# A gated linear attention's score levels joined in blocks of 1, 4 and 16 tokens, with two pieces of work moved in the queues

## The chip, the cores and the metric

The program runs on one core of one Trainium2 chip. The metric is the device time of one execution in microseconds; the kernel before has a median of 2559.4 us over 3 runs (2558.29 to 2559.68).

## The reference

The whole program is a retention layer, a latent-attention layer, a gated linear attention (GLA) layer with a feed-forward, all in float32. The change touches only the GLA mixer. It has 4 heads, a key width of 128 and a value width of 256 a head, and 1024 tokens:

```python
log_a = jax.nn.log_sigmoid(gk_low @ w_gk_up + b_gk) / 16.0
b = jnp.cumsum(gb, axis=-2)                                  # within a chunk
o_inter = jnp.einsum('bhck,bhkv->bhcv', qb * jnp.exp(b), state)
diff = b[:, :, :, None, :] - b[:, :, None, :, :]
decay = jnp.exp(jnp.where(causal[:, :, None], diff, -jnp.inf))
attn = jnp.einsum('bhik,bhjk,bhijk->bhij', qb, kb, decay)
o_intra = jnp.einsum('bhij,bhjv->bhiv', attn, vb)
k_dec = kb * jnp.exp(b_last - b)
state = state * jnp.exp(b_last) + jnp.einsum('bhck,bhcv->bhkv', k_dec, vb)
```

The kernel takes chunks of 128 tokens. The weight of query i on key j, i > j, is a sum over 128 key channels of q_i k_j exp(b_i - b_j). With a reference token m between them it is a plain product of q_i exp(b_i - b_m) and k_j exp(b_m - b_j), so pairs (i, j) are sorted by the reference token they share, and each sort is a matmul of its own.

## The kernel before

`gla_heads` (line 2074) gives one instruction stream to each of TensorE, VectorE, ScalarE, GpSimd and SyncE, joined by semaphores. `head(h, ...)` is run for the heads h = 0 to 3 (1 and 2 in a loop), and in it the steps t = 0 to 7, one for each chunk of 128 tokens; s = 8h + t. The order within a step is written out by hand.

TensorE (`tensor`, line 2632): in step t it runs `project_vr` of chunk t (24 matmuls of 512 columns, L2600), then `attend` of chunk s-3 (L2611 to L2614), then `scores` of chunk s-2 (L2622 to L2626). In step 4 the gate matmuls of the next head follow (L2580). After step 7 come four groups of 24 matmuls, `project_qk` (L2559), for the next head; the group g >= 2 reuses a bank and waits until ScalarE has copied group g-2 out. `attend(s)` waits for the chunk's weights (`mask_done`), for ScalarE to have copied out the output of chunk s-1 (`o_copied`), and for the state (`R_done`).

`scores` has 7 levels. At level l the 128 tokens of a chunk are cut into pairs of blocks of 2^l tokens, and the last token of the pair's first block is the reference; one 64-column matmul gives all pairs of that level (L2626). The diagonal is the column sum of q times k by a matmul with a matrix of ones (L2622), and the decayed keys are transposed (L2623).

VectorE (`vector`, line 2500): in each step `carry_state`, `gate`, `gather_weights` of chunk s-2, and then at most one or two pieces of the list below. `exponents(h, c)` forms the differences of b for one half c of a head (4 chunks, 512 tokens): 14 TENSOR_TENSOR of 256 elements and one of 512 (L2431 to L2434). ScalarE then runs `exponentials(h, c)` on them (L2260 to L2262), and `products(h, c)` multiplies by q and k (L2446 to L2450, 14 of 256 and 3 of 512). `gather_weights` copies the keys out of PSUM, puts the levels together by predicated copies into two tiles, even and odd, each copy waiting for the last but one, and adds the two tiles (L2475 to L2490).

The order of these pieces in VectorE: steps 0 and 1, `w_lower` (the lower part of a weight split) of pieces 0 and 1 of the next head; step 2, `up_lower`; step 3, `exponents(h, 1)`; step 4, `products(h, 1)`; steps 5 and 6, the gates of the next head; step 7, `exponents(h + 1, 0)`; after step 7, `w_lower` of pieces 2 to 5 and `products(h + 1, 0)`. In the last head steps 0 to 2 and 5 to 7 end instead with a call of `meanwhile`, which does weight splits of the closing stage (L3110 in VectorE, L3048 in ScalarE), one row block in each of the steps 0, 1 and 2.

ScalarE (`scalar`, line 2291): in each step `evacuate` of chunk s (copy of v, SiLU of the gate, L2277 and L2280) and `output` of chunk s-3 (copy of the output out of PSUM, L2287, and its squares, L2289); then `w_upper` in steps 0 and 1, `up_upper` in step 2, `exponentials(h, 1)` in step 3, `log_gates` in step 5, and in the last head `meanwhile` at the very end of a step. After step 7 it runs `w_upper(2)`, `qk_copy(0)`, `exponentials(h + 1, 0)`, `w_upper(3)`, `qk_copy(1)`, `w_upper(4)`, `qk_copy(2)`, `w_upper(5)`, `qk_copy(3)`. SyncE loads the raw weight pieces into two buffers; piece i waits until `w_lower` of piece i-2 is done.

## Time and profile before

| | |
|---|---|
| median of 3 runs | 2559.4 us |
| time of the profiled execution | 2557.12 us |
| span of the profiled execution | 2555.2 us |
| granted TensorE clock, mean | 0.999 |
| TensorE busy | 2523.7 us, 99% of the span |
| VectorE busy | 1220.6 us, 48% |
| ScalarE busy | 921.8 us, 36% |
| GpSimd busy | 466.2 us, 18% |
| mean DMA traffic | 76 GB/s |

The steps of the four GLA heads run from 1407 us to 1762 us of the span. The times of the rows below are microseconds from the start of the span.

### The profile page before, as it was taken

To read this page: it belongs to the slowest core of one execution; us is meant where nothing else is said; L and a number is where in the kernel's file an instruction comes from. 1 tells how busy PE (TensorE), PEld (TensorE's weight loads), DVE (VectorE), ACT (ScalarE), POOL (GpSimd) and SP (SyncE) were. 2 spreads that over 40 slices of the span, in tenths; PEclk is the share of its full clock that TensorE was granted. 3 is DMA by queue.
4 is the path that set the end of the run, shared out by engine and by line. 5 is a ranking of instruction groups with operands and counts; after the bars stand their busy time and mean duration, and the time that the engine had idled before them with its cause. 6 is when DMAs were issued, how large, how long until landed. Compare 5 with 4: busy or idle time off the path is not lost.

```text
span 2555.2 us, 34947 instructions
## 1 busy us (share of the span) xinstructions
PE 2523.7 (99%) x12568; PEld 2129.1 (83%) x12568; DVE 1220.6 (48%) x2485; ACT 921.8 (36%) x1840; POOL 466.2 (18%) x933
## 2 busy tenths in 40 slices
PE   8999999999999999999899999999999999999999
PEld 7888888888888987888788888888888888888887
DVE  4553634536423410577756767765443333333334
ACT  5443433424313422555544535443331122112212
POOL 3453534434000304322010101101000000000001
PEclk9999999999999999999999999999999999999999
DMA  5220211202533221222342111023341111111111
GB/s 212 78 76 21 92 39 58 73 18 93 194 115 106 69 91 52 61 60 60 97 162 99 42 59 45 31 79 110 110 141 40 50 57 41 49 46 61 33 49 75
DMA packets 76232, 194.48 MB, mean 76 GB/s; under 512 B 8528, under 2 KB 29392, under 8 KB 75344
## 3 DMA queue, kind: packets, MB, share of 16 engines
q1 hardware_dynamic: 76112, 192.85, 23.0%
q8 instruction: 79, 1.29, 0.2%
q14 instruction: 41, 0.34, 0.0%
HBM read 152.45 MB, written 36.18 MB: 74 GB/s over the span
## 4 chain that ended last, share of the span: by engine, by line
PE 57%; DVE 2%; ACT 1%; issue 1%; DMA 1%; DVEq 0%; POOL 0%; ACTq 0%; POOLq 0%; SPq 0%
PE wc_g_ps L3461 14%; PE wc_y_ps L3477 14%; PE gl_vr_ps L2600 7%; PE gl_j_ps L2559 3%; PE wb_y_ps L2928 3%; PE wc_y_ps L3210 3%; PE gl_l_ps L2626 2%; PE at_T_ps L1960 1%; PE at_j_ps L1912 1%; PE at_v_ps L1912 1%; PE at_v_ps L1913 1%; PE at_v_ps L1914 1%; PE at_s_ps L1914 1%; PE at_s_ps L1913 1%; PE at_s_ps L1912 1%
## 5 line engine op out<-in xcount | busy, mean ns | idle before, releaser
L3461 PE MATMUL wc_g_ps<-x_upper,ff_w1l 128*128 128x512 f32 x512 | 199.3, 389 | 0.0
L3461 PE MATMUL wc_g_ps<-x_upper,ff_w1h 128*128 128x512 f32 x512 | 199.2, 389 | 0.0
L3477 PE MATMUL wc_y_ps<-ff_w2h,ff_hl 128*128 128x512 f32 x512 | 199.2, 389 | 0.0
L3477 PE MATMUL wc_y_ps<-ff_w2l,ff_hh 128*128 128x512 f32 x512 | 199.2, 389 | 0.0
L3461 PE MATMUL wc_g_ps<-x_lower,ff_w1h 128*128 128x512 f32 x512 | 199.2, 389 | 0.0
L3477 PE MATMUL wc_y_ps<-ff_w2h,ff_hh 128*128 128x512 f32 x512 | 199.2, 389 | 0.0
L3415 DVE TENSOR_TENSOR ff_acc<-wc_y_ps,ff_acc 128x1024 f32<-128x1024 f32 x63 | 77.2, 1225 | 210.8 <-PE wc_y_ps L3477 210.8
L3340 ACT ACTIVATE ff_relu<-wc_g_ps 128x512 f32<-128x512 f32 x64 | 38.3, 598 | 378.8 <-PE wc_g_ps L3461 378.8
L3401 DVE SCALAR_TENSOR_TENSOR wc_g_ps<-wc_g_ps,ff_relu 128x512 f32<-128x512 f32 x64 | 44.8, 700 | 178.6 <-ACT ff_relu L3340 178.6
L3369 POOL TENSOR_SCALAR ff_ms<-ff_ss 128x1 f32<-128x1 f32 x8 | 1.8, 223 | 686.9 <-ACT x_lower L3357 686.0
L3477 PEld LDWEIGHTS wc_y_ps<-ff_w2l,ff_hh 128*128 128x128 f32 x512 | 96.1, 188 | 20.0
L3477 PEld LDWEIGHTS wc_y_ps<-ff_w2h,ff_hl 128*128 128x128 f32 x512 | 96.1, 188 | 20.0
L3461 PEld LDWEIGHTS wc_g_ps<-x_upper,ff_w1h 128*128 128x128 f32 x512 | 96.1, 188 | 20.0
L3461 PEld LDWEIGHTS wc_g_ps<-x_upper,ff_w1l 128*128 128x128 f32 x512 | 96.1, 188 | 19.9
L3461 PEld LDWEIGHTS wc_g_ps<-x_lower,ff_w1h 128*128 128x128 f32 x512 | 96.1, 188 | 19.9
L3477 PEld LDWEIGHTS wc_y_ps<-ff_w2h,ff_hh 128*128 128x128 f32 x512 | 96.1, 188 | 19.9
L1256 PE MATMUL ra_qkv_ps<-ra_wide_h,ra_xl 128*128 128x512 f32 x256 | 104.3, 407 | 8.1 <-DVE ra_wide_l L986 8.1
L1041 DVE TENSOR_TENSOR ra_sT<-ra_s_ps,ra_decay 128x128 f32<-128x128 f32 x64 | 18.6, 291 | 188.0 <-PE ra_s_ps L1295 188.0
L1256 PE MATMUL ra_qkv_ps<-ra_narrow_h,ra_xl 128*128 128x512 f32 x256 | 103.7, 405 | 0.0
L376 PE MATMUL wa_y_ps<-wa_wh,wa_gl 128*128 128x512 f32 x256 | 102.2, 399 | 0.8 <-DVE ra_vl L1061 0.6
L2600 PE MATMUL gl_vr_ps<-gl_vrh,x_lower 128*128 128x512 f32 x256 | 101.7, 397 | 0.0
L1256 PE MATMUL ra_qkv_ps<-ra_wide_h,ra_xh 128*128 128x512 f32 x256 | 101.3, 396 | 0.0
(433 smaller groups left out, 6992.0 us busy)
## 6 DMA issues: line engine op xcount, KB each, us to landing
staging<-in_w_ff SPq DMA_DIRECT2D x64, 512.0 KB, 3.8
...
```

Of the source, the lines that this page charges most:

```text
L376: last = pe.matmul(y_ps[slot][:, c, :], a[:, slot, kt, :], b[kt][:, c * HALF:(c + 1) * HALF], start=(kt == 0 and i == 0), stop=(kt == KW - ...
L1256: last = pe.matmul(out, a[:, kt, t * P:(t + 1) * P], b[:, kt, at:at + HALF], start=(kt == 0 and i == 0), stop=(kt == KT - 1 and i == 2))
L1912: pe.matmul(out, al, bh, start=start, stop=False)
L1913: pe.matmul(out, ah, bl, start=False, stop=False)
L1914: return pe.matmul(out, ah, bh, start=False, stop=stop)
L2559: last = pe.matmul(out, w[:, r, cols], xx[:, r, at], start=(r == 0 and i == 0), stop=(r == KT - 1 and i == 2))
L2600: last = pe.matmul(vr_ps[t % 2][:, :], xx[:, r, t * P:(t + 1) * P], w[:, r, :], start=(r == 0 and i == 0), stop=(r == KT - 1 and i == 2))
L2928: last = pe.matmul(y_ps[t % 2][:, c, :], a[t % 2][:, kt, :], b[kt][:, c * HALF:(c + 1) * HALF], start=(kt == 0 and i == 0), stop=(kt == KW ...
L3210: last = pe.matmul(y_ps[t % 2][:, c, :], a[t % 2][:, kt, :], b[kt][:, c * HALF:(c + 1) * HALF], start=(kt == 0 and i == 0), stop=(kt == KW ...
L3415: dve.tensor_tensor(acc[t][:, :], y_ps[t % 2][:, :, :].rearrange("p a n -> p (a n)"), acc[t][:, :], ALU.add).then_inc(y_added, 1)
L3461: last = pe.matmul(f_ps[j % 2][:, :], a[kt // 2][:, kt % 2, f * P:(f + 1) * P], b[:, kt, half * HALF:(half + 1) * HALF], start=(kt == 0 an ...
L3477: last = pe.matmul(y_ps[t % 2][:, n, :], a[:, f, t * P:(t + 1) * P], b[f][:, n * HALF:(n + 1) * HALF], start=(f == 0 and i == 0), stop=(f ...
```

## The change

Seven levels become three, of block size n = 1, 4 and 16. Each group of 4n tokens has three reference tokens, the last of its first, second and third block. The queries behind reference r are 3-r blocks, so that a level has 96 + 64 + 32 = 192 query columns a chunk, against 128 keys scaled to the end of their own block. At n = 1 the keys need no scale, so that the raw k is used. The last halving, 64 against 64 tokens, stays as it was (`halves`). The diagonal comes from a matmul of raw k and raw q. The chunks 4 to 7 use a copy of q and k (`own_qk`). `gather_weights` has 11 predicated copies in the place of 8. The last-token keys are the tile `gl_lv_rest[1]` and get their exponential in an instruction of their own. `exponents(h, 1)`, `exponentials(h, 1)` and `products(h, 1)` come one step earlier, and after step 7 the weight splits of pieces 2 and 3 stand ahead of `exponents(h + 1, 0)`.

```diff
-    NL = GLA_LEVELS
+    NL = len(GLA_BLOCKS)
+    BY_REF = (0, 96, 160)
+    QUERIES = 192
+    PARTS = 3 * NL + 2
+    LEVEL_AT = (P, P + QUERIES, 0)
+    HALVES_AT, KEYS_AT = QUERIES, QUERIES + GLA_HALF
+    MASK_AT = [3 * sum(P // (4 * m) for m in GLA_BLOCKS[:i]) for i in range(NL + 1)]
...
-    lv_main = [place(f"gl_lv{c}", [P, NL + 1, HALF], F32, at * KB) for c, at in enumerate((148, 112))]
+    EXPONENTS = NL * BT * QUERIES + (NL - 1) * HALF + HALF
+    lv_main = [place(f"gl_lv{c}", [P, EXPONENTS], F32, at * KB) for c, at in enumerate((148, 112))]
+    own_qk = [[place(f"gl_own_{n}{i}", [P, 2, P], F32, at) for i, at in enumerate(ats)]
+              for n, ats in (("q", (194 * KB, 148 * KB + 4 * EXPONENTS)), ("k", (76 * KB + 1568, 112 * KB + 4 * EXPONENTS)))]
     lv_rest = [place(f"gl_lv_rest{c}", [P, 2, HALF], F32, at * KB) for c, at in enumerate((164, 168))]
...
+    def queries(c, level):
+
+        at = level * BT * QUERIES
+        return lv_main[c][:, at:at + BT * QUERIES].rearrange("p (t n) -> p t n", t=BT)
+
+    def keys(c, level):
+
+        at = NL * BT * QUERIES + (level - 1) * HALF
+        return lv_main[c][:, at:at + HALF]
+
+    def halves(c):
+
+        return lv_main[c][:, EXPONENTS - HALF:EXPONENTS]
+    def own_chunk(src, t):
+
+        if t >= NT - 4:
+            return own_qk[src is k][t // 2 - 2][:, t % 2, :]
+        return src[:, t * P:(t + 1) * P]
+
+    def by_reference(c, level, r):
+
+        n = GLA_BLOCKS[level]
+        return queries(c, level)[:, :, BY_REF[r]:BY_REF[r] + 32 * (3 - r)].rearrange("p t (g x) -> p t g x", x=(3 - r) * n)
+
+    def behind_reference(src, level, r):
+
+        n = GLA_BLOCKS[level]
+        return src.rearrange("p (t g x) -> p t g x", t=BT, x=4 * n)[:, :, :, (r + 1) * n:]
...
         def exponentials(h, c):
             act.wait_ge(sub_done, 2 * h + c + 1)
-            act.activation(lv_main[c][:, :, :], lv_main[c][:, :, :], ACT.Exp, scale=INV_NORM)
+            act.activation(lv_main[c][:, :], lv_main[c][:, :], ACT.Exp, scale=INV_NORM)
+            act.activation(lv_rest[c][:, 1, :], lv_rest[c][:, 1, :], ACT.Exp, scale=INV_NORM)
             act.activation(lv_rest[c][:, 0, :], b[:, c * HALF:(c + 1) * HALF], ACT.Exp, scale=INV_NORM)
...
-                if t == 3:
+                if t == 2:
                     exponentials(h, 1)
                 if more and t == 5:
                     log_gates(h + 1)
                 if not more:
                     meanwhile(act, t)
             if more:
-                for g in range(4):
-                    w_upper(h + 1, 2 + g)
-                    qk_copy(h + 1, g)
-                    if g == 0:
-                        exponentials(h + 1, 0)
+                w_upper(h + 1, 2)
+                w_upper(h + 1, 3)
+                qk_copy(h + 1, 0)
+                w_upper(h + 1, 4)
+                exponentials(h + 1, 0)
+                qk_copy(h + 1, 1)
+                w_upper(h + 1, 5)
+                qk_copy(h + 1, 2)
+                qk_copy(h + 1, 3)
...
-                last = dve.tensor_tensor_scan(b[:, at], ones[:, :], mn[:, 0, at], 0.0, ALU.mult, ALU.add)
+                last = dve.tensor_tensor_scan(b[:, at], ones[:, :].broadcast_to([P, P]), mn[:, 0, at], 0.0, ALU.mult, ALU.add)
...
         def exponents(h, c, older):
-            for level in range(NL):
-                n = 1 << level
-                src = b[:, at].rearrange("p (g u n) -> p g u n", u=2, n=n)
-                dst = lv_main[c][:, level, :].rearrange("p (g u n) -> p g u n", u=2, n=n)
-                mid = src[:, :, 0, n - 1:n].broadcast_to([P, HALF // (2 * n), n])
-                dve.tensor_tensor(dst[:, :, 0, :], mid, src[:, :, 0, :], ALU.subtract)
-                dve.tensor_tensor(dst[:, :, 1, :], src[:, :, 1, :], mid, ALU.subtract)
+            for level, n in enumerate(GLA_BLOCKS):
+                if level:
+                    src = b[:, at].rearrange("p (g n) -> p g n", n=n)
+                    dve.tensor_tensor(keys(c, level).rearrange("p (g n) -> p g n", n=n),
+                                      src[:, :, n - 1:n].broadcast_to([P, HALF // n, n]), src, ALU.subtract)
+                for r in range(3):
+                    src = b[:, at].rearrange("p (t g x) -> p t g x", t=BT, x=4 * n)
+                    dve.tensor_tensor(by_reference(c, level, r), behind_reference(b[:, at], level, r),
+                                      src[:, :, :, (r + 1) * n - 1:(r + 1) * n].broadcast_to([P, BT, 32 // n, (3 - r) * n]),
+                                      ALU.subtract)
+            n = GLA_HALF
+            src = b[:, at].rearrange("p (t u n) -> p t u n", u=2, n=n)
+            dst = halves(c).rearrange("p (t u n) -> p t u n", u=2, n=n)
+            mid = src[:, :, 0, n - 1:n].broadcast_to([P, BT, n])
+            dve.tensor_tensor(dst[:, :, 0, :], mid, src[:, :, 0, :], ALU.subtract)
+            dve.tensor_tensor(dst[:, :, 1, :], src[:, :, 1, :], mid, ALU.subtract)
             src = b[:, at].rearrange("p (t n) -> p t n", n=P)
-            dve.tensor_tensor(lv_main[c][:, KD, :].rearrange("p (t n) -> p t n", n=P),
+            dve.tensor_tensor(lv_rest[c][:, 1, :].rearrange("p (t n) -> p t n", n=P),
                               src[:, :, P - 1:P].broadcast_to([P, BT, P]), src, ALU.subtract).then_inc(sub_done, 1)
...
         def products(h, c):
+                if level:
+                    dve.tensor_tensor(keys(c, level), keys(c, level), k[:, at], ALU.mult)
+                for r in range(3):
+                    dst = by_reference(c, level, r)
+                    dve.tensor_tensor(dst, dst, behind_reference(q[:, at], level, r), ALU.mult)
+            dst = halves(c).rearrange("p (t u n) -> p t u n", u=2, n=GLA_HALF)
+            for u, src in enumerate((k, q)):
+                dve.tensor_tensor(dst[:, :, u, :], dst[:, :, u, :],
+                                  src[:, at].rearrange("p (t u n) -> p t u n", u=2, n=GLA_HALF)[:, :, u, :], ALU.mult)
+            if c:
+                for src in (q, k):
+                    for i in range(2):
+                        dve.tensor_copy(own_qk[src is k][i][:, :, :],
+                                        src[:, HALF + 2 * i * P:HALF + 2 * (i + 1) * P].rearrange("p (t n) -> p t n", n=P))
+            dve.tensor_tensor(lv_rest[c][:, 1, :], lv_rest[c][:, 1, :], k[:, at], ALU.mult)
+            dve.tensor_tensor(lv_rest[c][:, 0, :], lv_rest[c][:, 0, :], q[:, at], ALU.mult).then_inc(mul_done, 1)
...
-            dve.tensor_copy(kt_[:, :], T_ps[:, P:2 * P])
-            for i, level in enumerate((0, None, 2, 1, 4, 3, 6, 5)):
-                dst, n = aT_parts[i % 2], 1 << (level or 0)
-                if i >= 2:
-                    dve.wait_ge(part_done, (NL + 1) * s + i - 1)
+            dve.tensor_copy(kt_[:, :], T_ps[:, KEYS_AT:KEYS_AT + P])
+            dve.copy_predicated(aT_parts[0][:, :], ident[:].bitcast(U32), l_ps[:, 0:P]).then_inc(part_done, 1)
+            dve.copy_predicated(aT_parts[1][:, GLA_HALF:], mask[:, MASK_AT[-1]:MASK_AT[-1] + 1].broadcast_to([P, GLA_HALF]),
+                                T_ps[:, HALVES_AT:HALVES_AT + GLA_HALF]).then_inc(part_done, 1)
+            i = 2
+            for level, n in enumerate(GLA_BLOCKS):
+                bank, groups = (l_ps, l_ps, T_ps)[level], P // (4 * n)
+                for r in range(3):
+                    dve.wait_ge(part_done, PARTS * s + i - 1)
                     wait_alone(dve)
-                if level is None:
-                    last = dve.copy_predicated(dst[:, :], ident[:].bitcast(U32), T_ps[:, 0:P])
-                else:
-                    last = dve.copy_predicated(
-                        dst[:, :].rearrange("p (g u n) -> p g u n", u=2, n=n)[:, :, 1, :],
-                        mask[:, level, :].rearrange("p (g n) -> p g n", n=n),
-                        l_ps[:, level * (P // 2):(level + 1) * (P // 2)].rearrange("p (g n) -> p g n", n=n))
-                last.then_inc(part_done, 1)
-            dve.wait_ge(part_done, (NL + 1) * s + NL + 1)
+                    at, x, w = LEVEL_AT[level] + BY_REF[r], (3 - r) * n, MASK_AT[level] + r * groups
+                    dve.copy_predicated(
+                        aT_parts[i % 2][:, :].rearrange("p (g x) -> p g x", x=4 * n)[:, :, (r + 1) * n:],
+                        mask[:, w:w + groups].unsqueeze(2).broadcast_to([P, groups, x]),
+                        bank[:, at:at + groups * x].rearrange("p (g x) -> p g x", x=x)).then_inc(part_done, 1)
+                    i += 1
+            dve.wait_ge(part_done, PARTS * s + PARTS)
             dve.tensor_tensor(aT[:, :], aT_parts[0][:, :], aT_parts[1][:, :], ALU.add).then_inc(mask_done, 1)
...
+                if t == 2:
+                    exponents(h, 1, older)
                 if t == 3:
-                    exponents(h, 1, older)
-                if t == 4:
                     products(h, 1)
                 if more and t == 5:
                     split_gates(h + 1)
                 if more and t == 6:
                     dve.wait_ge(exp_done, 2 * h + 2)
                     sum_gates(h + 1)
-                if more and t == 7:
-                    exponents(h + 1, 0, 1)
                 if not more:
                     meanwhile(dve, t)
             if more:
-                for i in range(2, PIECES):
-                    w_lower(h + 1, i)
+                w_lower(h + 1, 2)
+                w_lower(h + 1, 3)
+                exponents(h + 1, 0, 1)
+                w_lower(h + 1, 4)
+                w_lower(h + 1, 5)
                 products(h + 1, 0)
...
-            pe.matmul(T_ps[:, 0:P], ones[:, :], lv_rest[c][:, 1, at], start=True, stop=True)
-            pe.transpose(T_ps[:, P:2 * P], lv_main[c][:, KD, at], ident[:])
+            qc, kc = own_chunk(q, t), own_chunk(k, t)
+            pe.transpose(T_ps[:, KEYS_AT:KEYS_AT + P], lv_rest[c][:, 1, at], ident[:])
+            pe.matmul(l_ps[:, 0:P], kc, qc, start=True, stop=True)
             for level in range(NL):
-                n = 1 << level
-                last = pe.matmul(l_ps[:, level * (P // 2):(level + 1) * (P // 2)].rearrange("p (g n) -> p g n", n=n),
-                                 lv_main[c][:, level, at],
-                                 lv_main[c][:, level, at].rearrange("p (g u n) -> p g u n", u=2, n=n)[:, :, 1, :],
-                                 start=True, stop=True)
+                pe.matmul((l_ps, l_ps, T_ps)[level][:, LEVEL_AT[level]:LEVEL_AT[level] + QUERIES],
+                          keys(c, level)[:, at] if level else kc, queries(c, level)[:, t % BT, :], start=True, stop=True)
+            last = pe.matmul(T_ps[:, HALVES_AT:HALVES_AT + GLA_HALF], halves(c)[:, at],
+                             halves(c)[:, t % BT * P + GLA_HALF:(t % BT + 1) * P], start=True, stop=True)
             last.then_inc(score_mm, 1)
...
@@ -3043,6 +3111,7 @@
             act.wait_ge(gl.b_done, GLA_HEADS + 1)
         if kt == 3:
             act.wait_ge(gl.mul_done, 2 * GLA_HEADS)
+            act.wait_ge(gl.score_mm, GLA_HEADS * NT - 4)
```

## Rows read from the trace of the kernel before

**Rows 1.** Busy time in the stretch of the GLA steps; then granted clock, DMA.

```profile
1407.00:1762.00 355.00, 355.00 (x1857) 305.30 (x1855) 246.09 (x735) 161.64 (x291) 39.52 (x62) 1.00 0.16 51
```

**Rows 2.** Chain of waits, in order of time: start, length.

```profile
1606.22 1.51 PE gl_l_ps L2626 x14
```

**Rows 3.** Timeline of TensorE, last step of head 1: start, length.

```profile
1557.53 0.59 PE L2614 MATMUL gl_k_ps<-gl_v,gl_kt__9814 128*128 128x256 f32 x2
1557.96 0.38 PE L2622 MATMUL gl_T_ps<-gl_lv_rest,gl_ones 128*128 128x128 f32 x2
1558.18 0.27 PE L2623 MATMUL gl_T_ps<-ident,gl_lv 128*128 128x128 f32 x1
1558.29 1.67 PE L2626 MATMUL gl_l_ps<-gl_lv 128*128 128x64 f32 x14
```

**Rows 4.** Timeline of VectorE, head 2: gathering the weights of chunk 0.

```profile
1607.86 0.29 DVE L2475 COPY gl_kt__9814<-gl_T_ps 128x128 f32<-128x128 f32 x1 [1.06 <-PE gl_l_ps L2626]
...
1608.20 0.30 DVE L2482 COPY_PREDICATED gl_aT_odd<-ident,gl_T_ps 128x128 f32<-128x128 uint32 x1
1608.46 0.23 DVE L2484 COPY_PREDICATED gl_aT_even<-gl_mask,gl_l_ps 128x64 f32<-128x64 uint32 x1
...
1609.65 0.29 DVE L2490 TENSOR_TENSOR gl_aT<-gl_aT_even,gl_aT_odd 128x128 f32<-128x128 f32 x1
1609.86 0.34 DVE L2361 SCALAR_TENSOR_TENSOR gl_up<-gl_up_high,gl_parts,gl_up_raw 96x128 fp32r<-96x128 f32 x1
```

**Rows 5.** Timeline of VectorE, head 2: the end of the exponents.

```profile
1622.57 0.42 DVE L2432 TENSOR_TENSOR gl_lv<-gl_b 128x256 f32<-128x256 f32 x1
1622.91 0.68 DVE L2434 TENSOR_TENSOR gl_lv<-gl_b 128x512 f32<-128x512 f32 x1
1623.51 0.47 DVE L2459 SCALAR_TENSOR_TENSOR gl_R<-gl_R,gl_last_decay,gl_k_ps 128x256 f32<-128x256 f32 x1
```

**Rows 6.** Timeline of ScalarE, head 2, steps 3 and 4.

```profile
1623.63 3.63 ACT L2260 ACTIVATE gl_lv<-gl_lv 128x4096 f32<-128x4096 f32 x1 [7.24 <-DVE gl_lv L2434]
1627.16 0.61 ACT L2261 ACTIVATE gl_lv_rest<-gl_b 128x512 f32<-128x512 f32 x1
...
1627.78 0.36 ACT L2277 ACTIVATE gl_v<-gl_vr_ps 128x256 f32<-128x256 f32 x1
...
1629.72 0.38 ACT L2287 ACTIVATE gl_oS<-gl_o_ps 128x256 f32<-128x256 f32 x1
```

**Rows 7.** Timeline of TensorE, head 2: the output matmul of steps 4 and 5.

```profile
1621.34 0.38 PE L2611 MATMUL gl_o_ps<-gl_v,gl_aT 128*128 128x256 f32 x1
...
1630.43 0.38 PE L2611 MATMUL gl_o_ps<-gl_v,gl_aT 128*128 128x256 f32 x1
```

**Rows 8.** Groups of VectorE in the closing stage, whole run: count, busy, mean ns.

```profile
L3131 DVE TENSOR_SCALAR wc_xn<-wc_y,wc_rx 128x1024 f32<-128x1024 f32 x8 | 6.0, 754 | 17.0 <-POOL wc_rx L3106 17.0
```

**Rows 9.** Timeline of VectorE, after step 7 of head 1.

```profile
1560.10 0.29 DVE L2475 COPY gl_kt__9814<-gl_T_ps 128x128 f32<-128x128 f32 x1 [1.06 <-PE gl_l_ps L2626]
...
1567.40 1.40 DVE L2368 SCALAR_TENSOR_TENSOR gl_vrl<-staging,gains,gl_vrh 128x512 fp32r<-128x512 f32 x2
```

**Rows 10.** Timeline of TensorE: the fourth group of projections begins.

```profile
1576.20 0.39 PE L2559 MATMUL gl_j_ps<-x_upper,gl_qkl 128*128 128x512 f32 x1
```

**Rows 11.** Timeline of ScalarE, last head, step 2: a weight split.

```profile
1697.88 1.13 ACT L3048 ACTIVATE wc_wh<-staging,gains 128x1024 fp32r<-128x1024 f32 x1
```

**Rows 12.** Timeline of VectorE, last head: chunk 0 gathered, then a split.

```profile
1698.99 0.29 DVE L2475 COPY gl_kt__9814<-gl_T_ps 128x128 f32<-128x128 f32 x1 [1.06 <-PE gl_l_ps L2626]
...
1700.95 1.28 DVE L3110 SCALAR_TENSOR_TENSOR wc_wl<-staging,gains,wc_wh 128x1024 fp32r<-128x1024 f32 x1
```

**Rows 13.** Timeline of TensorE, last head, step 4: the output matmul.

```profile
1712.46 0.59 PE L2611 MATMUL gl_o_ps<-gl_v,gl_aT 128*128 128x256 f32 x2
```

**Rows 14.** Timeline of VectorE: the last chunk's weights added.

```profile
1760.04 0.29 DVE L2490 TENSOR_TENSOR gl_aT<-gl_aT_even,gl_aT_odd 128x128 f32<-128x128 f32 x1
```

**Rows 15.** Timeline of TensorE: the last output matmul.

```profile
1760.81 0.38 PE L2611 MATMUL gl_o_ps<-gl_v,gl_aT 128*128 128x256 f32 x1
```

58 lines of the change are left out of this document (27 added, 31 removed).

## The prediction

> **What bounds the kernel now.** I read the table of the profile first: TensorE is busy 99% of the span. The view of busy time by stretch says it more sharply for the steps that the change touches: TensorE is busy 355.00 of 355.00 us, at a granted clock of 1.00, and VectorE 246.09, ScalarE 161.64 [rows 1]. So TensorE never waits there, and every microsecond that its own work gets shorter would show, unless another engine becomes late. What the reader has to take from the timelines is therefore how late each engine is: the slack of each wait of TensorE. It is small in places. In head 2 ScalarE ends the copy of an output at 1629.72 + 0.38 = 1630.10, and the matmul that waits for it starts at 1630.43 [rows 6, 7].
>
> **What TensorE saves.** Starts tell the price of one matmul, since the lengths overlap. 14 instructions of 64 columns take 1.51 us [rows 2], 0.108 each, and a float32 matmul is two of them: 0.216 us. 128 columns take 1558.18 - 1557.96 = 0.22, 256 columns 1557.96 - 1557.53 = 0.43, the transpose, one instruction, 0.11 [rows 3]. So 64 and 128 columns cost the same, and from there on it is 1.68 ns a column; 192 columns I put at 0.32 (ends: 0.22 and 0.43, the rows at either side). A set of scores was 0.22 + 0.11 + 1.51 = 1.83 us. It will be 0.11 (transpose) + 0.22 (q on k) + 3 x 0.32 + 0.22 (the halves) = 1.50. That is 0.33 less, 32 times: **-10.7 us** (with the ends for 192 columns, -20 to -0.3; the two-sided interpolation leaves little doubt, so I keep 1 us either way).
>
> The Trainium skill, page "TensorE: Matmul & The Clock Gate", section "Step-by-step: what each phase is for", says that throughput is purely the number of moving columns. By that rule the new scores would cost more: 128 + 128 + 576 + 64 = 896 columns against 128 + 128 + 448 = 704. The rows on 64 and 128 columns, at the same price, do not agree with it for this float32 form.
>
> **What VectorE pays.** 256 elements take 0.34 from start to start, 512 take 0.60 [rows 5]: 0.07 + 1.035 ns an element. Exponents: a level has 384 + 256 + 128 = 768 elements in three instructions, the second and third level 512 more for keys, then 2 x 256 and 512: 14 instructions, 4352 elements, 5.5 us (before: 14 x 0.336 + 0.60 = 5.3). Products: 15 instructions, 4864 elements, 6.1 us (before 6.5); in the second half four copies of 256 more. A copy is bounded by the 0.34 of a two-operand instruction and by 754 ns for 1024 elements with one operand in SBUF, 0.19 [rows 8]; I take 0.2, near the row of its own kind: 6.9.
>
> The Trainium skill, page "VectorE: DVE Perf Modes", section "The perf-mode tier table (the rule you actually need)", gives a float32 copy within SBUF twice the rate of a two-operand instruction. Reading all four at 0.34 instead would add 0.5 us once, in the last head.
>
> Gathering: before, 0.60 for the first three instructions, then six waiting copies from 1608.46 to 1609.65, 0.198 each, and 0.21 for the addition, 2.0 in all [rows 4]. The new one has the same three in front, then nine waiting copies of 96, 64 or 32 elements, 64 in the mean: 0.60 + 9 x 0.19 + 0.21 = 2.55. Ends: the nine at 0.13 (1607.86 to 1608.20, less 0.21 for the copy in front: a 64-element one that waits for nothing) give 2.0; at 0.26 (1608.20 to 1608.46, 128 elements), 3.15.
>
> **What ScalarE pays.** Exponentials took 1627.78 - 1623.63 = 4.15 [rows 6]. 256 elements less at (3.63 - 0.61) / 3584 = 0.84 ns are -0.2, one more instruction of 512 is +0.5: 4.45.
>
> **The move to step 2, heads 0 to 2.** I walk from the start of the gathering in step 2, 1607.86. VectorE: 2.55 gathering, 0.25 `up_lower` (a row of 0.34, less the overlap) [rows 4], 5.5 exponents, so 8.3 later. ScalarE needs 0.1 to begin (1623.51 to 1623.63) and 4.45: 12.85. Behind it stands `evacuate`, with its table load, 1629.72 - 1627.78 = 1.94, and then the output copy, 0.38: 15.2. The matmul that waits for this copy stands in step 4, at 1621.34 [rows 7], 13.48 after the start, now 0.33 sooner since one set of scores lies between: 13.15. With 0.1 to restart, **TensorE waits 2.1 us**. Before, one step later, the same copy ended 0.3 ahead of its matmul. Of the 2.4 between, 0.33 are the shorter scores, 0.55 the gathering, 0.25 `up_lower`, 0.2 the exponents, 0.3 the exponentials; the other 0.8 is a shorter way for TensorE, as chunk 0 in step 3 has no state matmul (0.43, 256 columns) and the next head's gates, two matmuls, only follow in step 4. Nothing pays it back, as TensorE is the bound: **3 x 2.1 = +6.3 us.**
>
> **The last head.** Here step 2 ends with `meanwhile`, and the move puts it behind the long work: ScalarE's `w_upper` (1.13 [rows 11]) stands behind the exponentials, and VectorE's `w_lower`, which waits for it, stands ahead of the next gathering. From 1698.99 [rows 12]: 2.55 + 5.5 + 0.1 + 4.45 + 1.13 = 13.7, `w_lower` 1.2, `carry_state` and `gate` 0.8 (two of 0.47, less the overlap [rows 5]), gathering 2.55: 18.3. Its matmul was at 1712.46 [rows 13], less 0.33: 13.15 after the start. **TensorE waits 5.2 us.** Next on VectorE come the products, 6.9, then 0.8 and 2.55: 28.6. TensorE, from 18.4, does 1.3 of attending, 1.5 of scores and 5.45 to 5.55 of projections: 26.7. **1.9 us more.** Sum +7.1.
>
> **The end of a head.** From 1560.10 [rows 9]: 2.55, two splits at 1.33 (a pair of 1.40 less the overlap, [rows 9]), exponents 5.5, 0.1, exponentials 4.45, the copy of k 0.5: 15.8. The fourth projection group needs it at 1576.20 [rows 10], 16.1 after. Slack 0.3: nothing, but every 0.1 beyond that counts three times. The last weight split follows this copy: 15.8 + 1.3 for its upper part (taken as long as the lower) + 1.4 = 18.5, needed 5.5 after 16.1; 3 us to spare. The transfers of raw pieces 4 and 5 wait for the splits that end 3.9 and 5.2 after the start, where the first ended 8.7 after it before (1568.80); they start sooner, and no store stands between them. At the very end, the last sum is done at 1760.33 and needed at 1760.81 [rows 14, 15]; 0.48 less 0.55 and the restart: +0.2.
>
> The rest (addresses, the smaller mask, the scan's one broadcast column) I cost at nothing. The opening keeps its order, and no instruction of it that TensorE can wait for grows by more than the 0.3 of the exponentials, the end for it. The new wait for `score_mm` in the last head's step 5 holds ScalarE until that step's scores, 1.5 us after the attending that it waits for anyway; behind it stands the evacuation of step 6, which comes 5.5 us later.
>
> **Sum:** -10.7 + 6.3 + 7.1 + 0.2 = **+2.9 us**. On the profiled execution, span 2555.2 and 2557.12 of time, that is 2560.0; it lies 2.3 below the median of the runs, and against the median it is 2559.4 + 2.9 = **2562.3 us**. About 0.2%, 5.1 us, is what a measurement of this kernel can tell from no change; 2.9 is within it.
>
> **Rivals.**
> (1) *The gathering and the many-stride instructions of VectorE cost more than their elements say.* The short waiting copies may be held by their semaphores, and three nested strides with runs of 1 to 3 elements are in no row. Each 0.1 in the gathering adds 3 x 0.1 + 0.2 + 0.1 in the stalls named, and 3 x 0.1 at the fourth projection group once its 0.3 is gone. At 2.9, with exponents at 6.0, the three stalls are 3.0, the last head 9.2, the projections 3 x 0.6, the end 0.6: +9.9, 2569.3. Against it: the 15 instructions of the exponents before, with runs from 1 to 64 elements, all keep to the line. It decides from 0.3 more gathering on. Chance of ending slower by over 5.1: 0.35.
> (2) *Faster: VectorE is quick enough that the stalls shrink.* If the short copies fall to 0.15 (gathering 2.2) and the exponents to 4.9, the walk of heads 0 to 2 is 0.95 shorter, 3 x 1.15, and the last head 2.3 shorter, 4.8: -10.7 + 3.5 + 4.8 = -2.4, still within 5.1. To pass -5.1 the last head's 5.2 must not come about either, for instance because the split's upper part reaches ScalarE ahead of the exponentials; the listing speaks against it. Then -10.7 + 3 x 1.7 = -5.6, 2553.8. Chance 0.15.
> (3) *Scores by the column.* If 192 columns cost more than the line (0.43, as 256), the saving is nearly gone: +13, 2572.6. It is part of the slower 0.35, at 0.03.
> (4) *The stalls don't come, -10.7, 2548.7.* The before-walk, which ends within 0.3 us of the trace, speaks against it; 0.05 of the 0.15.
>
> **How the numbers follow.** My forecast, both stalls as worked out, has 0.50: no change that can be told. Faster 0.15, slower 0.35. The unknown costs add up to about -5 and +7; the range takes in rival 1 whole and most of rival 2: 2552 to 2572. The likeliest case's own range is 2558 to 2564.5.
>
> **What would show it.** Scores start to start 1.50 instead of 1.83. In TensorE's waits, about 2.1 us at L2611's successor in step 4 of each of heads 0 to 2, released by the output copy of ScalarE; two waits in the last head, about 5 and 2 us, released by the sum of the two tiles on VectorE. No wait at the projections. The gathering 2.55 from its first copy to its end, exponents 5.5, exponentials 4.45. I am wrong if the waits are absent with these durations as said (then an order of mine is misread), or if gathering takes 2.9 or more (then rival 1).

## The result, and the profile after

| | before | after |
|---|---|---|
| median of 10 runs each, us | 2558.32 (2556.82 to 2559.68) | 2565.97 (2563.72 to 2567.13) |
| time of the profiled execution, us | 2557.12 | 2566.14 |
| span of the profiled execution, us | 2555.2 | 2564.3 |
| mean granted TensorE clock | 0.999 | 0.996 |

The kernel became slower: the ratio is 1.0028, 95% interval [1.002, 1.0037], or +7.65 us between the medians. The forecast was +2.9 and "no change that can be told". The time lies in the range of 2552 to 2572, but outside the likeliest case's own range of 2558 to 2564.5: of the three cases, "slower" came, to which the prediction gave 0.35.

The table of engines first, of the kernel after:

```profile
PE 2519.7 (98%) x12376; PEld 2119.5 (83%) x12376; DVE 1241.5 (48%) x2573; ACT 923.7 (36%) x1848; POOL 465.7 (18%) x933
```

TensorE has 4 us less to do and the span is 9 us longer. So something now waits. The same stretch as [rows 1], a little longer since the stage ends later (columns as there), and TensorE's own waits in it (us in total, times, longest):

```profile
1407.00:1780.00 373.00, 360.00 (x1708) 303.02 (x1707) 270.88 (x830) 167.16 (x305) 40.75 (x66) 0.99 0.17 56
```

```profile
PE gl_o_ps L2679 <- issue: 6.6, 3, 2.3
PE gl_o_ps L2679 <- DVE gl_aT L2557: 5.5, 2, 5.4
```

L2679 is the output matmul that was L2611. It waits in step 4 of each head and once more in step 5 of the last one. The five rows of TensorE's timeline (in brackets the idle time in front and its releaser):

```profile
1441.66 0.67 PE L2679 MATMUL gl_o_ps<-gl_v,gl_aT 128*128 128x256 f32 x2 [2.00 <-issue]
...
1532.57 0.67 PE L2679 MATMUL gl_o_ps<-gl_v,gl_aT 128*128 128x256 f32 x2 [2.31 <-issue]
...
1625.42 0.99 PE L2679 MATMUL gl_o_ps<-gl_v,gl_aT 128*128 128x256 f32 x2 [2.32 <-issue]
...
1721.34 1.22 PE L2679 MATMUL gl_o_ps<-gl_v,gl_aT 128*128 128x256 f32 x2 [5.37 <-DVE gl_aT L2557]
...
1731.67 0.70 PE L2679 MATMUL gl_o_ps<-gl_v,gl_aT 128*128 128x256 f32 x2 [0.15 <-DVE gl_aT L2557]
```

"issue" names no releaser. ScalarE's timeline in head 2 does: its output copy (L2331) stands last behind the exponentials, as the prediction had it, ends at 1624.94 + 0.38 = 1625.32, and the matmul starts at 1625.42.

```profile
1618.54 3.42 ACT L2303 ACTIVATE gl_lv<-gl_lv 128x3840 f32<-128x3840 f32 x1 [7.89 <-DVE gl_lv_rest L2491]
...
1623.00 0.36 ACT L2321 ACTIVATE gl_v<-gl_vr_ps 128x256 f32<-128x256 f32 x1
1623.37 1.28 ACT L2324 ACT_TABLE_LOAD   x1
...
1624.94 0.38 ACT L2331 ACTIVATE gl_oS<-gl_o_ps 128x256 f32<-128x256 f32 x1
```

The windows of one microsecond behind the wait of head 1 (the two left out show 0.50 as well), and one of 6 us behind each of the three longer waits (the number behind the five engines is the granted clock), show what the prediction did not have:

```profile
1532.50:1533.50 1.00, 0.93 (x4) 0.87 (x5) 1.00 (x4) 0.99 (x4) 0.33 (x1) 0.99 0.00 0
1533.50:1534.50 1.00, 1.00 (x4) 0.68 (x3) 1.00 (x4) 0.06 (x1) 1.00 (x1) 0.50 0.06 16
...
1536.50:1537.50 1.00, 1.00 (x7) 0.96 (x6) 1.00 (x3) 0.00 (x0) 1.00 (x1) 0.80 0.00 0
1537.50:1538.50 1.00, 1.00 (x6) 0.82 (x5) 0.68 (x2) 0.00 (x0) 0.83 (x3) 1.00 0.00 0
...
1624.50:1630.50 6.00, 5.08 (x20) 4.37 (x21) 6.00 (x17) 2.76 (x10) 4.39 (x2) 0.72 0.00 0
...
1720.00:1726.00 6.00, 4.66 (x18) 4.02 (x19) 5.96 (x20) 0.92 (x4) 1.07 (x2) 0.72 0.49 157
...
1441.60:1443.60 2.00, 1.94 (x11) 1.77 (x12) 2.00 (x7) 1.42 (x5) 1.34 (x1) 1.00 0.00 0
```

After the wait of 2.31 us TensorE restarts at full clock, falls to 0.50 (1.2 of 2.4 GHz) about 1 us later, and is back after some 3.4 us of work at that level: 3 x 0.50 + 0.20 = 1.7 us lost. The waits of 2.32 and 5.37 us cost the same by their 6 us windows (6 x 0.28 = 1.7). After the wait of 2.00 us, in head 0, the clock stays at 1.00. This is one execution; two kernels below show that the same waits do not always bring the same falls.

**Where the time went.** From the first projection of the stage to its last state matmul the kernel before took 1407.08 to 1761.67, the one after 1408.25 to 1770.68: +7.8 us. Of the other 1.3 us of the 9.1 between the spans, 1.2 lie ahead of the stage: in front of the matmul at 1272 us TensorE waits in both kernels for VectorE, and behind this wait the clock fell in the profiled execution of the changed kernel (wait 3.02 us; mean clock 0.79 from 1272 to 1280) and not in that of the kernel before (wait 2.37 us; 1.00). Of the eleven kernels below, eight have this fall in their profiled execution and three do not, on either side with the old levels as with the new, so that it is not put down to the change.

The terms in the stage: scores 32 x -0.33 = -10.6; the five waits +12.15; three falls of the clock 3 x 1.7 = +5.1; 0.3 at the fourth projection group in two of the three head changes, which also starts late; and 0.3 at the last output matmul, also a little late. Sum +7.5 of 7.8.

### The profile page after: what moved, and what is told of

Read it like the earlier page. It is cut to its first block, busy times and chain, and to the rows that moved or that the text cites. A ratio compares the mean times of both kernels' runs of the same rounds, so it can differ in the third digit from the quotient of the medians.

```text
span 2564.3 us, 34803 instructions
## 1 busy us (share of the span) xinstructions
PE 2519.7 (98%) x12376; PEld 2119.5 (83%) x12376; DVE 1241.5 (48%) x2573; ACT 923.7 (36%) x1848; POOL 465.7 (18%) x933
## 4 chain that ended last, share of the span: by engine, by line
PE 56%; DVE 3%; issue 1%; ACT 1%; DMA 1%; DVEq 0%; POOL 0%; ACTq 0%; POOLq 0%; SPq 0%
PE wc_g_ps L3530 14%; PE wc_y_ps L3546 14%; PE gl_vr_ps L2668 6%; PE wb_y_ps L2996 3%; PE wc_y_ps L3279 3%; PE gl_j_ps L2627 3%; PE at_T_ps L1961 1%; PE gl_l_ps L2694 1%; PE at_j_ps L1913 1%; PE at_v_ps L1913 1%; PE at_v_ps L1914 1%; PE at_v_ps L1915 1%; PE at_s_ps L1915 1%; PE at_s_ps L1914 1%; PE at_s_ps L1913 1%
## 5 line engine op out<-in xcount | busy, mean ns | idle before, releaser
L1257 PE MATMUL ra_gate_ps<-ra_wide_h,ra_xl 128*128 128x512 f32 x256 | 100.2, 391 | 0.6 <-DVE ra_wide_l L987 0.6
```

The costliest lines, as they stand in the source:

```text
L1257: last = pe.matmul(out, a[:, kt, t * P:(t + 1) * P], b[:, kt, at:at + HALF], start=(kt == 0 and i == 0), stop=(kt == KT - 1 and i == 2))
```

## The experiments

Each kernel was run 5 to 11 times, between runs of the kernel before (21 or 22) on the same chip; times are medians in us, ratios stand with 95% intervals, and a difference is to the kernel before on that chip. All compute the whole reference, but for two that do more than it, as said there.

**The halves, each alone.** First the long pieces put back (`exponents(h, 1)`, `exponentials(h, 1)` in step 3, `products(h, 1)` in step 4), with the moved splits kept:

```diff
@@ scalar
-                if t == 2:
+                if t == 3:
                     exponentials(h, 1)
@@ vector
-                if t == 2:
-                    exponents(h, 1, older)
                 if t == 3:
+                    exponents(h, 1, older)
+                if t == 4:
                     products(h, 1)
```

> The changed kernel with exponents(h, 1), exponentials(h, 1) and products(h, 1) back in steps 3, 3 and 4; new levels and moved splits stay. Theory A (the move puts ScalarE's output copy and, in the last head, a weight split behind the long exponentials, and TensorE waits for them; where it has waited over 2.3 us its clock falls as well): the waits of 2.0 to 2.3 us in step 4 and the 5.4 us in the last head go. In their place come short waits in steps 5 and 7, about 1.2 us each by the walk with the durations of the changed kernel, 1.7 in the last head, all too short for the clock to fall: 9 us of waits against 10.7 saved, -1.5 us against before (range -4 to +1), and a granted clock of 1.00 throughout. Theory B (the new levels themselves are too dear for VectorE, the order matters little): still +5 to +8 us against before.

Measured: 2557.51 us against 2558.39, ratio 0.9997 [0.9988, 1.0006].

Then both moves put back, which leaves the new levels alone:

```diff
@@ vector, besides the edit above
+                if more and t == 7:
+                    exponents(h + 1, 0, 1)
...
-                w_lower(h + 1, 2)
-                w_lower(h + 1, 3)
-                exponents(h + 1, 0, 1)
-                w_lower(h + 1, 4)
-                w_lower(h + 1, 5)
+                for i in range(2, PIECES):
+                    w_lower(h + 1, i)
@@ scalar
-                w_upper(h + 1, 2)
-                w_upper(h + 1, 3)
-                qk_copy(h + 1, 0)
-                w_upper(h + 1, 4)
-                exponentials(h + 1, 0)
-                qk_copy(h + 1, 1)
-                w_upper(h + 1, 5)
-                qk_copy(h + 1, 2)
-                qk_copy(h + 1, 3)
+                for g in range(4):
+                    w_upper(h + 1, 2 + g)
+                    qk_copy(h + 1, g)
+                    if g == 0:
+                        exponentials(h + 1, 0)
```

> Only the new levels; both moves undone. Theory A: as the kernel with the second half back, plus about 1.0 us at the first projections of values in each of three heads, since the last weight split of a head is late again (it had 0.4 us to spare before and gathering is 0.7 longer): +1.5 us against before (range -1 to +4). Theory B (levels too dear): +5 to +8 us. Rival on the splits (their move is worth nothing): the same as with the second half back, within 0.5 us.

Measured: 2561.2 against 2558.39, ratio 1.0011 [1.0002, 1.002].

Then the kernel before, with its seven levels, in the new order:

```diff
@@ scalar of the kernel before
-                if t == 3:
+                if t == 2:
                     exponentials(h, 1)
@@ vector of the kernel before
-                if t == 3:
+                if t == 2:
                     exponents(h, 1, older)
-                if t == 4:
+                if t == 3:
                     products(h, 1)
```

and the splits in the order of the changed kernel.

> The kernel before with its 7 levels, and both moves of the change. Theory A: waits of about 0.8 us in step 4 of heads 0 to 2, of 3.3 and 0.6 us in the last head; the 3.3 us let the clock fall, some 1.7 us more: +8 us against before (range +5 to +9). Theory B (the order is harmless, the levels cost): within 1 us of before.

Measured: 2566.49 against 2558.39, ratio 1.0032 [1.002, 1.0045]. TensorE's waits in the profiles of the three, in this order:

```profile
PE gl_o_ps L2679 <- issue: 7.6, 7, 1.4
...
PE gl_o_ps L2679 <- DVE gl_aT L2557: 0.3, 2, 0.2
```

```profile
PE gl_o_ps L2674 <- issue: 7.5, 7, 1.4
PE gl_vr_ps L2663 <- DVE gl_vrl L2412: 2.6, 3, 1.0
```

```profile
PE gl_o_ps L2616 <- DVE gl_aT L2494: 3.1, 1, 3.1
PE gl_o_ps L2616 <- issue: 1.7, 3, 0.6
```

Three things follow. The new levels do not bring their 10.6 us in the old order either: the same matmul then waits one step later, in step 5, and again in step 7, seven times by 0.98 to 1.41 us and twice by 0.16. So ScalarE has no slack left, whichever of the two steps the exponentials are in. It had 0.33 us in step 5 before [rows 6, 7]; the scores are 0.33 shorter, and what stands ahead of its copy is longer by 0.5 (gathering), 0.3 (exponents) and 0.3 (exponentials), by the durations given further down: 1.1 us late, where 1.0 was seen in heads 0 to 2. With the new levels the old place is the better one by 7.65 + 0.88 = 8.5 us. Second, with the old levels the move costs 8.1 us by itself, with waits of only 4.8 us in the profile; the last of them, 3.05 us, is followed by a clock of 0.69 over 5 us, 1.6 us lost:

```profile
1720.00:1725.00 5.00, 5.00 (x25) 4.43 (x25) 5.00 (x15) 0.89 (x3) 1.25 (x1) 0.69 0.45 158
```

In the profiled executions the stage is 361.85 us long against 354.59, 7.3 more, which leaves 0.9 that no row names. The rest of the 8.1 may lie outside the stage: the stage starts 1.6 us later than in the kernel before, since at 985 us, long before the stage, TensorE was at half clock for 6.8 us instead of 3.4. Third, without the moved splits the first projections of the next head wait for the last weight split (L2663, 0.67, 1.00 and 0.90 us), which they don't with them.

**The last head alone put back.**

```diff
@@ scalar
-                if t == 2:
+                if t == (2 if more else 3):
                     exponentials(h, 1)
@@ vector
-                if t == 2:
+                if t == (2 if more else 3):
                     exponents(h, 1, older)
-                if t == 3:
+                if t == (3 if more else 4):
                     products(h, 1)
```

> The changed kernel, but in the last head alone exponents(h, 1), exponentials(h, 1) and products(h, 1) stand in steps 3, 3 and 4 again. Theory A (the last head pays 5.4 us of waiting and about 1.7 us of clock, since a weight split stands behind the exponentials): its wait becomes the 1.4 us seen with the second half back everywhere; +1.9 us against before (range +0.5 to +3.5), so 5.8 us less than the change. Rival (the last head is a head like the others, at 2.3 us of waiting and 1.7 of clock): about 2.6 us less than the change, +5 against before.

Measured: 2560.84 against 2558.95, ratio 1.0006 [0.9997, 1.0015]: +1.9, the +1.9 that was expected. Its four waits, of 2.01 (head 0), 2.31, 2.33 and 1.41 us, are

```profile
PE gl_o_ps L2679 <- issue: 8.1, 4, 2.3
```

By the medians the last head's share of the change is so 7.65 - 1.9 = 5.8 us: 5.52 of waits and 1.7 of clock, less the 1.41 that takes their place. That it comes out to the tenth is luck, since the runs of this kernel lie between 2557.72 and 2562.71. The expectation had two falls of the clock; the profiled execution (2562.53) has three, the first behind the wait of 2.01 us in head 0:

```profile
1442.50:1448.50 6.00, 5.98 (x24) 5.36 (x25) 5.68 (x17) 1.90 (x7) 5.21 (x3) 0.72 0.00 0
```

**The splits alone put back** (the part of the second experiment's edit that concerns them, with the long pieces left in steps 2 and 3).

> The changed kernel with the weight splits of pieces 2 and 3 behind exponents(h + 1, 0) again. Theory A (gathering and the exponents are longer, so the last split of each of heads 1 to 3 comes late): waits of 0.7 to 1.0 us at the first projection of values in three heads, +2.5 us on top of the change, +10.2 against before. Rival (the split's move has no worth, as TensorE never waited for it before): +7.7, as the change.

Measured: 2567.39 against 2558.95, ratio 1.0035 [1.0023, 1.0048]; +8.4 where +10.2 was expected. The waits at the next head's projections come back as said,

```profile
PE gl_vr_ps L2663 <- DVE gl_vrl L2412: 2.5, 3, 1.0
```

but by the medians the move of the splits is worth 8.4 - 7.65 = 0.8 us, not 2.5. The profiled spans (2566.1 - 2564.3 = 1.8) do not settle it, since the two executions differ in their falls of the clock. Here the wait of 2.33 us in head 2 was followed by none, where the changed kernel had one behind 2.32:

```profile
1627.20:1633.20 6.00, 5.88 (x30) 5.18 (x31) 5.67 (x17) 1.97 (x8) 5.11 (x3) 1.00 0.00 0
```

In the last head the stretch at half clock was twice as long, 0.57 over 1721 to 1729. The first two experiments differ by the same edit, and neither of their profiled executions has a fall in the stage: from the first projection to the last state matmul they take 357.10 and 354.46 us, 2.6 apart (by the medians 3.7). The waits say 2.5 less the 0.6 at the fourth group, 1.9. So the move is worth some 2 to 2.6 us; the medians scatter too widely (4 us between the six runs of this experiment) to say more.

**The clock term by itself.** To tell the wait from the clock, TensorE is kept busy where it would wait: ahead of the output matmul in step 4 it computes products that nobody reads, after the previous state has been taken out. They are work beyond the reference's.

```diff
-        def attend(s, t, older):
+        def attend(s, t, older, fill_with=0):
...
+            if fill_with:
+                pe.wait_ge(R_done, s)
+                for _ in range(fill_with):
+                    pe.matmul(k_ps[:, :], xh[:, 0, 0:P], xl[:, 0, 0:HALF], start=True, stop=True)
...
-                    attend(s - 3, before(h, t, 3)[1], older or t >= 4)
+                    attend(s - 3, before(h, t, 3)[1], older or t >= 4, (9 if more else 23) if t == 4 else 0)
```

> The changed kernel with matmuls of 512 columns that nobody reads, put into the time in which TensorE waits before the output matmul of step 4: 9 of them (2.04 us at 0.227) in heads 0 to 2, 23 (5.2 us) in the last. Their result goes to the bank of the state product, once that was read. The work is useless; if idleness is what lets the clock fall, it costs nothing and keeps the clock. Theory A (the wait of 2.3 us or more lets TensorE's clock fall to half for some 3.4 us after it, 1.7 us lost in each of heads 1 and 2; in the last head VectorE's products set the next wait, so that nothing is gained there): granted clock 1.00 in the stretches 1530 to 1545 and 1620 to 1635, 3.4 us faster than the changed kernel, +4.3 against before. Rival (the slow stretch has another cause, or the filling only lengthens the wait): the clock falls all the same, and the time stays at +7.7 or rises.

Measured: 2565.08 against 2558.95, ratio 1.0023 [1.0014, 1.0033]; +6.1 where +4.3 was expected. In heads 1 and 2 it did what it was meant to:

```profile
1530.00:1545.00 15.00, 14.70 (x73) 12.12 (x72) 11.96 (x39) 6.82 (x17) 6.68 (x6) 1.00 0.05 16
1620.00:1635.00 15.00, 14.68 (x72) 12.00 (x71) 11.29 (x37) 6.86 (x19) 5.93 (x4) 1.00 0.03 9
```

The clock is 1.00 where the changed kernel had 0.89 in the same stretches. In the last head the filling was misplaced. The state it has to wait for is itself held behind ScalarE's split, so that it began late and ran too long:

```profile
1715.37 5.51 PE L2678 MATMUL gl_k_ps<-x_lower,x_upper 128*128 128x512 f32 x23 [2.46 <-DVE gl_R L2521]
1720.72 0.59 PE L2683 MATMUL gl_o_ps<-gl_v,gl_aT 128*128 128x256 f32 x2
```

From the last matmul's end to the output matmul 2.46 + 5.35 = 7.8 us pass instead of 5.37, 2.4 more, which takes the gain of the fall that is gone here too (1.7) and more. This profiled execution has no fall in the whole stage and, at 2562.96, is the second fastest of the eleven; what the median has above it, 2.1 us, no trace shows. So the same was run with the filling in heads 0 to 2 alone (`9 if more else 0`):

> As the filled kernel, but with the 9 unread matmuls in heads 0 to 2 only; the last head as in the changed kernel. Theory A (the clock's fall after the wait costs 1.7 us in each of heads 1 and 2, and the last head of the filled kernel lost some 2.5 us because its filling began only after the state was carried): clock 1.00 in heads 0 to 2, 3.4 us less than the change: +4.3 us against before (range +3 to +5.5). Rival (the clock costs next to nothing): +7.7.

Measured: 2563.85 against 2558.48, ratio 1.0021 [1.0012, 1.003]: +5.4 where +4.3 was expected; against the +7.65 of the change 2.3 less, where two falls make 3.4. By the medians alone the two kernels cannot be told apart, as their intervals to the kernel before overlap; the traces can tell them. From head 0's output matmul in step 4 to the last head's one it takes 1717.93 - 1441.10 = 276.83 us; in the changed kernel it was 1721.34 - 1441.66 = 279.68. That is 2.85 less, with both waits filled by as much time as they had taken, so it is the clock's. And in the last head, where nothing was edited, the stretch at half clock came out twice as long in this execution, with the same wait of 5.37 us. It began some 0.8 us ahead of the restart at 1717.93, while TensorE still waited, and ended at 1724.0, 6.1 us behind the restart:

```profile
1716.00:1724.00 8.00, 6.07 (x18) 5.40 (x19) 7.96 (x28) 1.51 (x6) 2.76 (x3) 0.57 0.41 132
...
1717.00:1718.00 1.00, 0.07 (x1) 0.07 (x1) 0.97 (x5) 0.00 (x0) 0.05 (x1) 0.59 0.73 212
```

The next output matmul comes 1729.30 - 1717.93 = 11.37 us later, in the changed kernel 10.33 (of which 0.15 is a wait): 1.2 us more without that wait. A fall after a long wait costs therefore 1.7 us in one execution and some 3 in another (6.1 us at half clock).

Whether the filling is what kept the clock up has to be asked over all of these executions, since a wait of some 2 us can pass without a fall by itself. In step 4 of heads 0 to 2 the changed kernel and the two kernels above (the last head alone, the splits alone put back) have nine waits of 2.00 to 2.33 us, and six of them were followed by half clock. The two filled kernels have these places filled, six in all, and none was.

**Only ScalarE's piece behind its output copy.** The exponents stay early in VectorE, the exponentials go to step 3 behind that step's output copy, the products to step 4:

```diff
@@ scalar
-                if t == 2:
+                if t == 3:
                     exponentials(h, 1)
@@ vector
-                if t == 3:
+                if t == 4:
                     products(h, 1)
```

> The changed kernel with VectorE's exponents(h, 1) left in step 2, but ScalarE's exponentials(h, 1) in step 3, behind that step's output copy, and products(h, 1) in step 4. Theory A: no wait in steps 4 and 5 and none at the last head's split; 0.6 us in step 7 of heads 0 to 2 (the gates of the next head), 0.4 at the very end: -8.4 us against before (range -10 to -6), clock 1.00. Theory B (VectorE is the limit): slower than before or equal, with waits of TensorE released by the sum of the two tiles.

Measured: 2549.18 against 2558.39, ratio 0.9965 [0.9951, 0.9979]. ScalarE's timeline in head 2 says why:

```profile
1611.23 0.38 ACT L2331 ACTIVATE gl_oS<-gl_o_ps 128x256 f32<-128x256 f32 x1 [0.20 <-PE gl_k_ps L2682]
...
1613.66 3.42 ACT L2303 ACTIVATE gl_lv<-gl_lv 128x3840 f32<-128x3840 f32 x1 [0.21 <-DVE gl_lv_rest L2491]
...
1620.21 0.38 ACT L2331 ACTIVATE gl_oS<-gl_o_ps 128x256 f32<-128x256 f32 x1
```

In the changed kernel ScalarE stood still for 7.89 us in front of the exponentials, until VectorE had their input, with step 3's evacuation and output copy behind them. Here this copy comes first (the row of 1611.23), 6.4 us ahead of its matmul at 1618.05; the exponentials then wait 0.21, and step 4's copy, at 1620.21, is as early for its matmul at 1626.80. The only waits left are three of 0.2 to 0.4 us, in step 7:

```profile
PE gl_o_ps L2679 <- issue: 0.9, 3, 0.4
```

**The rest of the waits.** To the version just shown, the next head's `log_gates` is added one step later:

```diff
-                if more and t == 5:
+                if more and t == 6:
                     log_gates(h + 1)
```

> The changed kernel with exponentials(h, 1) behind the output copy of step 3, products(h, 1) in step 4, and log_gates(h + 1) in step 6 instead of 5. Theory A: the last waits of TensorE in the heads, 0.2 to 0.4 us in step 7 behind ScalarE's gates, go as well, about 0.9 us less than with log_gates in step 5: -10 us against before (range -11.5 to -9). Rival (VectorE, which needs the gates' logarithm in step 6, becomes late instead): no gain over the -9.2, waits released by the sum of the tiles.

Measured: 2549.48 against 2558.95, ratio 0.9965 [0.9952, 0.9979]. The waits of step 7 are gone, and the time has come back at the fourth projection group (0.26, 0.51 and 0.50 us), whose bank ScalarE's copy of k frees:

```profile
PE gl_j_ps L2627 <- ACT gl_k L2313: 1.3, 3, 0.5
```

That copy stands behind the exponentials, and these behind two weight splits of VectorE. With one of the two behind the exponents again, on top of this:

```diff
                 w_lower(h + 1, 2)
-                w_lower(h + 1, 3)
                 exponents(h + 1, 0, 1)
+                w_lower(h + 1, 3)
```

> The kernel with the gates in step 6, and VectorE's split of piece 3 behind exponents(h + 1, 0), that of piece 2 ahead. Theory A (every step of the chain gathering, two splits, exponents, exponentials, copy of k counts at the fourth projection group, which waits 0.3 to 0.5 us there): that wait goes, as the chain is 1.3 us shorter, and the last split has about 3 us to spare, of which it takes a part: 1.2 us less than with the gates in step 6 alone, -10.5 us against before (range -12 to -9.5), no wait of TensorE in the heads. Rival (the later split of piece 3 delays the load of piece 5, and the wait moves to the first projection of values): -8.5 or less gained.

Measured: 2548.1 (2547.12 to 2548.8) against 2558.48, ratio 0.996 [0.9946, 0.9973], -10.4 where -10.5 was expected. This version is faster than both kernels. Its two waits in the stage are 0.5 us in all, and from the first projection to the last state matmul it takes 1407.49 to 1752.05, 344.56 against 354.59 before: -10.0 of the scores' -10.6.

**The order without the levels.** To see whether the good order is worth anything by itself, the kernel before, with seven levels, in the order of the version with ScalarE's piece behind its output copy (exponents in step 2, the splits moved in VectorE and ScalarE, exponentials and products where they were; ScalarE's part of the edit is left out here):

```diff
@@ vector of the kernel before
-                if t == 3:
+                if t == 2:
                     exponents(h, 1, older)
...
-                if more and t == 7:
-                    exponents(h + 1, 0, 1)
...
-                for i in range(2, PIECES):
-                    w_lower(h + 1, i)
+                w_lower(h + 1, 2)
+                w_lower(h + 1, 3)
+                exponents(h + 1, 0, 1)
+                w_lower(h + 1, 4)
+                w_lower(h + 1, 5)
```

> The kernel before with its 7 levels, in the order of the best version so far: VectorE's exponents(h, 1) in step 2, its products in step 4, ScalarE's exponentials in step 3 behind the output copy, and the splits of pieces 2 and 3 moved. Theory A (TensorE never waited before, so an order can give it nothing; the 9 us come from the new levels alone): within 1 us of before. Rival (the order is worth something by itself): 3 us or more faster than before.

Measured: 2558.46 against 2558.48, ratio 1.0002 [0.9993, 1.0011]. TensorE has no wait in the heads, as before. The order gives nothing without the levels, and the levels give nothing without the order (the second experiment: +2.8).

## Why the prediction was right and where it was wrong

**The scores: right.** The last scores of head 2 ahead of the gathering (start, length):

```profile
1608.03 0.27 PE L2691 MATMUL gl_T_ps<-ident,gl_lv_rest 128*128 128x128 f32 x1
1608.14 0.39 PE L2692 MATMUL gl_l_ps<-gl_q,gl_k 128*128 128x128 f32 x2
1608.36 0.49 PE L2694 MATMUL gl_l_ps<-gl_lv,gl_k 128*128 128x192 f32 x2
1608.69 0.49 PE L2694 MATMUL gl_l_ps<-gl_lv 128*128 128x192 f32 x2
1609.02 0.49 PE L2694 MATMUL gl_T_ps<-gl_lv 128*128 128x192 f32 x2
1609.34 0.33 PE L2696 MATMUL gl_T_ps<-gl_lv 128*128 128x64 f32 x2
...
1609.48 0.48 PE L2668 MATMUL gl_vr_ps<-gl_vrh,x_lower 128*128 128x512 f32 x1
```

192 columns take 0.33 from start to start (put at 0.32), and the set 1609.48 - 1608.03 = 1.45 to the next matmul, whose length of 0.48 is 0.09 above that of its kind: between 1.45 and 1.54, where 1.50 was forecast and 1.83 was before [rows 2, 3]. From the output matmul of step 4 to that of step 5 it takes 1626.80 - 1618.05 = 8.75 in the version with ScalarE's piece later, where neither waits, and 1630.43 - 1621.34 = 9.09 before [rows 7]: 0.34 less. Rival 3, that the price goes by the column, is out. The 192-column rows lie on the line that the rows of 128 and 256 columns gave. (One end of the prediction's range has a wrong sign: at 0.43 for 192 columns a set would be 0.11 + 0.22 + 1.29 + 0.22 = 1.84, so that the end would be +0.3 in all and not -0.3.)

**VectorE's and ScalarE's durations: right, so rival 1 is not what made it slower.** The gathering of chunk 0 in head 2 runs from 1609.81 to 1612.38 + 0.2, 2.77, of which about 0.2 is the first copy's own start after an idle stretch; in the last head it takes 1721.20 - 1718.67 = 2.53 (put at 2.55; rival 1 needed 2.9, and exponents of 6.0). A predicated copy is about 0.19 again:

```profile
1609.81 0.29 DVE L2540 COPY gl_kt__9818<-gl_T_ps 128x128 f32<-128x128 f32 x1 [0.70 <-PE gl_T_ps L2696]
...
1610.63 0.30 DVE L2551 COPY_PREDICATED gl_aT_even<-gl_mask,gl_l_ps 128x96 f32<-128x96 uint32 x1
1610.80 0.30 DVE L2551 COPY_PREDICATED gl_aT_odd<-gl_mask,gl_l_ps 128x64 f32<-128x64 uint32 x1
...
1612.38 0.29 DVE L2557 TENSOR_TENSOR gl_aT<-gl_aT_even,gl_aT_odd 128x128 f32<-128x128 f32 x1
...
1612.85 1.18 DVE L2481 TENSOR_TENSOR gl_lv<-gl_b 128x384 f32<-128x384 f32 x3
...
1617.83 0.68 DVE L2491 TENSOR_TENSOR gl_lv_rest<-gl_b 128x512 f32<-128x512 f32 x1
1618.43 0.41 DVE L2521 COPY gl_R<-gl_k_ps 128x256 f32<-128x256 f32 x1
```

The exponents take 1618.43 - 1612.85 = 5.58 (put at 5.5), the exponentials 1623.00 - 1618.54 = 4.46 (4.45). The products of the second half take 7.0 (6.9), with the two copies of 256 elements at 0.2 each:

```profile
1726.19 0.49 DVE L2512 COPY gl_own_q<-gl_q 128x256 f32<-128x256 f32 x2
```

**The move to step 2: right in kind and in size.** Three waits of 2.1 were forecast, 2.00, 2.31 and 2.32 came: 6.63 against 6.3, at the place and behind the copy named.

**The last head: the first wait right, the second not.** 5.2 forecast, 5.37 measured, by the chain forecast: exponentials, then `w_upper`, then `w_lower` with the gathering behind it.

```profile
1715.58 1.13 ACT L3117 ACTIVATE wc_wh<-staging,gains 128x1024 fp32r<-128x1024 f32 x1
```

```profile
1716.75 1.28 DVE L3179 SCALAR_TENSOR_TENSOR wc_wl<-staging,gains,wc_wh 128x1024 fp32r<-128x1024 f32 x1 [5.66 <-ACT wc_wh L3117]
...
1720.99 0.29 DVE L2557 TENSOR_TENSOR gl_aT<-gl_aT_even,gl_aT_odd 128x128 f32<-128x128 f32 x1
```

The matmul starts at 1721.34, 0.15 behind that sum.

The second, 1.9 forecast, was 0.15. VectorE was as late as the prediction said; TensorE was late too, since half clock took 1.7 us in this step. So this fall cost 1.7 and covered 1.75 of a wait, and the sum for the last head, +7.1 forecast, is 5.37 + 1.7 + 0.15 = 7.2.

**The step that failed** is the sentence "With 0.1 to restart, TensorE waits 2.1 us" and the sum 3 x 2.1 behind it: a wait was priced at its own length plus a restart. In the profiled execution those of 2.31 us and more cost their length and 1.7 us of clock behind them. In heads 1 and 2 that is 2 x 1.7 = +3.4 that the sum did not have (in the last head it changed places with the second wait, in head 0 it did not occur). With the 0.3 that the waits were longer, and 0.6 for the fourth projection group, whose slack of 0.3 I had called enough, the forecast's +2.9 becomes +7.3, against +7.65 measured. The term is not a fixed one: behind waits of 2.00 to 2.33 us there were two falls in the three heads here, three in one kernel above and one in another, 1.7 us each, and the runs of the changed kernel lie 3.4 us apart (2563.72 to 2567.13). That the time lies in the stated range of 2552 to 2572 is in part luck: the room above 2564.5 was made for rival 1, whose cost did not come, and no term or rival had the clock.

The Trainium skill, page "TensorE: Matmul & The Clock Gate", section "What's actually happening", says that the array runs at half rate by default and that activity releases it. The trace agrees in that the low level is half, 0.50, and stands behind waits.

**The rival of no stalls** (-10.7, 2548.7) had 0.05, and as a forecast for the change it was rightly small. But it is the time that the levels are worth, and the runs show how it is had: 2548.1 with ScalarE's piece behind the output copy.
